# A decoder layer whose projections are moved between its expert steps: one tile in front, four and three behind

## The reference

```python
h = rms_norm(x, norm1_w) * (1 + sc1) + sh1            # sc, sh, g from silu(c) @ w_ada + b_ada
z = h @ w_in                                          # 1024 x 6656
q, k, v, u, gate_post, gate_pre, g_attn, g_conv = jnp.split(z, IN_SPLITS, axis=-1)
q, k = rms_norm(q, q_norm_w), rms_norm(k, k_norm_w)   # per head
o_attn = attend(q, k, v, sinks)                       # window of 128
conv_y = short_conv(gate_pre * u, conv_prev, conv_w, conv_bias)
merged = sigmoid(g_attn) * o_attn + sigmoid(g_conv) * (gate_post * conv_y)
x = x + g1 * (merged @ w_out)
h2 = rms_norm(x, norm2_w) * (1 + sc2) + sh2
x = x + g2 * peer_ffn(h2)                             # per token 8 heads x 16 rows of expert_u, expert_v
```

## Time and profile before

| | us |
|---|---|
| median of 3 runs | 3891.65 (3890.81 to 3892.19) |
| profiled execution, its own time | 3892.44 |
| its span | 3890.4 |
| PE busy | 3279.5 (84%) |
| DVE busy | 2530.7 (65%) |
| POOL busy | 2407.8 (62%) |
| ACT busy | 1077.4 (28%) |
| moved by DMA | 1259.47 MB, 324 GB/s over the span |

### The profile page before, as it was taken

How to read it: one execution, slowest core, us unless ns; L and a number is a source line. 1 busy time by engine, 2 the same in 40 slices (tenths; PEclk the granted TensorE clock), 3 DMA queues, 4 the chain that set the end, 5 groups by cost and what they waited for, 6 DMA issues and landing times.

```text
span 3890.4 us, 35676 instructions
## 1 busy us (share of the span) xinstructions
PE 3279.5 (84%) x10638; PEld 1724.2 (44%) x10638; DVE 2530.7 (65%) x5905; ACT 1077.4 (28%) x2400; POOL 2407.8 (62%) x2146
## 2 busy tenths in 40 slices
PE   4899995997999999999978778867887788789777
PEld 1457773444555655566534233423342334334221
DVE  2355546666887776787746677667766876776663
ACT  1225551222322322243212223213221323222220
POOL 1000003777667777766757777777777777776775
PEclk7999998999999999999989999999999999999999
DMA  6452225999999999999999999999999999999998
GB/s 217 160 172 71 60 60 186 345 373 382 367 356 371 385 384 351 390 353 348 357 392 363 370 358 351 363 358 365 372 365 360 372 369 376 368 374 336 370 364 316
DMA packets 466874, 1259.47 MB, mean 324 GB/s; under 512 B 42071, under 2 KB 171415, under 8 KB 466014
## 3 DMA queue, kind: packets, MB, share of 16 engines
q0 software_dynamic: 304128, 1107.43, 76.0%
q1 hardware_dynamic: 141290, 136.46, 10.7%
q10 hardware_dynamic: 21268, 13.32, 1.1%
HBM read 1238.54 MB, written 20.55 MB: 324 GB/s over the span
## 4 chain that ended last, share of the span: by engine, by line
PE 32%; DMA 25%; POOL 20%; DVE 9%; issue 9%; ACT 5%; SPq 0%; DVEq 0%; ACTq 0%; POOLq 0%
PE bank L1746 19%; DMA v_ring<-in_expert_v_dram,idx 18%; POOL u_ring L674 10%; POOL v_ring L682 10%; PE bank L1574 6%; DMA u_ring<-in_expert_u_dram,idx 5%; DVE u_ring L1349 2%; PE bank L1715 2%; PE bank L1770 1%; PE bank L1696 1%; DMA mod_s<-mod 1%; PE bank L1553 1%; ACT sm L768 1%; DVE rt L1132 1%; ACT sm L777 1%
## 5 line engine op out<-in xcount | busy, mean ns | idle before, releaser
L1746 PE MATMUL bank<-v_ring,diag 128*128 128x512 f32 (+1 forms) x4224 | 2068.8, 620 | 487.4 <-DMA v_ring<-in_expert_v_dram,idx 389.5
L1349 DVE CUSTOM_DVE_ANT_0 u_ring<-u_ring,h2b 128x1024 f32<-128x1024 f32 x1056 | 1286.8, 1225 | 877.7 <-DMA u_ring<-in_expert_u_dram,idx 835.9
L674 POOL DMA_INDIRECT u_ring<-in_expert_u_dram,idx x1056 | 1186.2, 1123 | 767.9 <-DVEq L1330 393.3
L682 POOL DMA_INDIRECT v_ring<-in_expert_v_dram,idx x1056 | 1206.4, 1142 | 475.1 <-PE bank L1746 239.9
L1746 PEld LDWEIGHTS bank<-v_ring,diag 128*128 128x128 f32 (+1 forms) x4224 | 754.0, 192 | 1555.6 <-DMA v_ring<-in_expert_v_dram,idx 830.5
L920 ACT ACTIVATE diag<-ident,wgt 128x128 f32<-128x128 f32 x1024 | 357.3, 394 | 664.2 <-PE bank L1746 310.1
L1574 PE MATMUL bank<-hi,whi 128*128 128x512 f32 x832 | 413.1, 497 | 2.4 <-issue 2.4
L1574 PE MATMUL bank<-hi,wlo 128*128 128x512 f32 x832 | 328.9, 395 | 0.0
L1574 PE MATMUL bank<-lo,whi 128*128 128x512 f32 x832 | 327.6, 394 | 0.0
L1126 DVE TENSOR_TENSOR wlo<-wc,whi 128x1024 fp32r<-128x1024 f32 x104 | 127.4, 1226 | 123.2 <-ACT whi L733 117.6
L1574 PEld LDWEIGHTS bank<-hi,whi 128*128 128x128 f32 x832 | 159.0, 191 | 75.5 <-issue 51.2
(11 more groups left out here) (259 smaller groups left out, 2607.4 us busy)
## 6 DMA issues: line engine op xcount, KB each, us to landing
wc<-in_w_in_dram SPq DMA_DIRECT2D x104, 512.0 KB, 5.9
ada_w<-in_w_ada_dram SPq DMA_DIRECT2D x12, 2048.0 KB, 8.1
u_ring<-in_expert_u_dram,idx POOLq DMA_INDIRECT x1056, 6.4
v_ring<-in_expert_v_dram,idx POOLq DMA_INDIRECT x1056, 6.4
wo_sb<-in_w_out_dram SPq DMA_DIRECT2D x2, 4096.0 KB, 19.1
wq_sb<-in_w_query_dram SPq DMA_DIRECT2D x2, 4096.0 KB, 28.1
xt<-in_x_prompt_dram SPq DMA_DIRECT2D x8, 512.0 KB, 4.9
out_dram<-h2b SPq DMA_DIRECT2D x8, 512.0 KB, 6.9
```

Source lines behind the costliest of these rows:

```text
L674: pool.indirect_dma_start(out=u_ring[k % RING][:, :], out_offset=None, in_=eu, in_offset=bass.IndirectOffsetOnAxis(ap=idx[n % IDXS][:, k:k ...
L682: pool.indirect_dma_start(out=v_ring[k % RING][:, :], out_offset=None, in_=ev, in_offset=bass.IndirectOffsetOnAxis(ap=idx[n % IDXS][:, k:k ...
L1349: V.tensor_tensor_reduce(out=u_ring[k % RING][:, :], in0=u_ring[k % RING][:, :], in1=h2b[t % 2][:, :], scale=1.0, scalar=0.0, op0=ALU.mult ...
L1746: last = M(banks(c, 1)[0:parts, :], diag[k % DIAGS][:, 0:parts], v_ring[k % RING][:, c * 512:(c + 1) * 512], start=first, stop=final)
```

## The change

The tiles are cut otherwise: tile 0 alone in front, then tiles 1 to 4, then tiles 5 to 7 together with the samples.

- **Front.** The first two sixths of the modulation are computed as columns (`modulation_columns`, four blocks of `w_ada` as stationary operand, 9 moving columns). Tile 0 is transposed before scale and shift. Its projection runs with its tokens stationary and the weights moving, 512 output columns at a time: 13 column blocks (`COLS1`), each of two units of 1 MB (`load_unit`, a ring of 3, split by `split_unit`), 12 matmuls a unit. The other eight `w_ada` blocks run one behind each of the first eight column blocks. The results are transposed back by `transpose_job`. Eight head pairs of attention, tile 0's convolution and the norms and transposes of tiles 1 to 4 run beside the column blocks 6 to 12.
- **Tiles 1 to 4** (group 0): the 52 blocks run in slots 0 to 69, one in 1.35 slots, all 24 matmuls in one slot. The weights have a ring of 3.
- **Tiles 5 to 7 and the samples** (group 1): the 52 blocks run in slots 280 to 558, one in 5.45 slots, in four pieces, with 416 moving columns; the separate 32-column matmuls are gone.
- **Attention** of tile 1 begins at slot 24, then 84, 142, 190, 500, 642, 770; the output steps of tiles 1 to 8 at 78, 142, 187, 233, 579, 690, 818, 930. Tiles 1 to 7 all go through DRAM for queries, keys, values and gates. Parked second inputs are those of tiles 3 and 4.
- `w_out` and `w_query` are loaded three times: at the end of the front, at slot 71 and at slot 571.

The core of the diff:

```diff
+COLS = 4
+HALF = KC // 2
+NUNIT = 2 * IN_W // ABLK
+UNIT_RING = 3
 NPROJ = QKV // P + 5 * KC
-NORMED = NQK // 2
...
-P2_LOAD = 98
-P2_SPLIT = 102
-P2_FIRST = 112
-P2_PITCH = 6.0
-A_MID = 330
-A_PITCH = 5
-MERGE_MID = 433
...
+GROUPS = ((1, 2, 3, 4), (5, 6, 7))
+NPT = tuple(len(g) * P for g in GROUPS)
+NTOK = (NPT[0], NPT[1] + NS)
+GMAX = max(NTOK)
...
+P_FIRST = (0, 280)
+P_PITCH = (1.35, 5.45)
+P_LOAD = (0, 266)
+NORM_AT, NORM_STEP = 266, 3
+WO_AT = (71, 571)
+ATTN = (None, 24, 84, 142, 190, 500, 642, 770)
+A_PITCH = (None, 4, 5, 4, 4, 5, 5, 5)
+MERGE = (None, 77, 135, 184, 231, 577, 688, 816)
+D_BASE = (None, 78, 142, 187, 233, 579, 690, 818, 930)
...
+SPLIT_HI, SPLIT_LO = (-3, -6), (-2, -4)
+PIECES = ((0,), (0, 1, 3, 4))
+SQUARE, MEANS, ROOT, NORM, PARK = (1, 5), (2, 6), (2, 7), (3, 8), (4, 10)
+BY_ACT, BY_DVE, TAPS, GATE, PARK_Y = (1, 5), (2, 6), (2, 7), (2, 7), (3, 9)
...
+        COLS1 = [("q", 0), ("q", 1), ("kv", 0), ("u", 0), ("pre", 0), ("u", 1), ("pre", 1),
+                 ("gc", 0), ("post", 0), ("gc", 1), ("post", 1), ("ga", 0), ("ga", 1)]
...
+            def load_unit(u):
+                if u >= UNIT_RING:
+                    sp.wait_ge(u_split, u - UNIT_RING + 1)
+                kind, c = COLS1[u // 2]
+                cols = slice(FIRST_COL[kind] + c * ABLK, FIRST_COL[kind] + c * ABLK + ABLK)
+                sp.dma_start(wu[u % UNIT_RING][:, :, :], w_in_v[:, u % 2 * HALF:u % 2 * HALF + HALF, cols]
+                             ).then_inc(wu_in[u % UNIT_RING], 16)
...
+            for i in range(len(COLS1)):
+                for u in (2 * i + 3, 2 * i + 4):
+                    if u < NUNIT:
+                        load_unit(u)
+                j = COLS - 1 + i
+                if COLS <= j < NBLK:
+                    if COLS + 2 <= j + 1 < NBLK:
+                        sp.wait_ge(mod_stored, 32 * (j - COLS))
+                        load_bias(j + 1)
+                    store_mod(j)
+                    if j + 2 < NBLK:
+                        load_ada(j + 2)
+                if i == 1:
+                    load_xt(1)
...
+            sp.wait_ge(u_split, NUNIT)
+            sp.wait_ge(pT_ps, KC)
+            sp.dma_start(wo_first[:, :, :], w_out_v).then_inc(wo_in, 16)
+            sp.wait_ge(unit_ps, NUNIT)
+            sp.dma_start(wq_first[:, :, :], w_query_v).then_inc(wq_in, 16)
...
+                for g in range(2):
+                    if s == WO_AT[g]:
+                        sp.wait_ge(proj_ps, (g + 1) * NPROJ)
+                        sp.dma_start(wo_sb[:, :, :], w_out_v).then_inc(wo_in, 16)
+                        if g:
+                            sp.wait_ge(new_stored, 32)
+                        sp.dma_start(wq_sb[:, :, :], w_query_v).then_inc(wq_in, 16)
+                        sp.wait_ge(gated, (g + 1) * KC)
...
+            def split_unit(u):
+                w(wu_in[u % UNIT_RING], 16 * (u // UNIT_RING + 1))
+                if u >= UNIT_RING:
+                    w(unit_ps, u - UNIT_RING + 1)
+                nc.scalar.copy(uhi[u % UNIT_RING][:, :, :], wu[u % UNIT_RING][:, :, :]).then_inc(uhi_made, 1)
...
+            for i in range(len(COLS1) + 1):
+                m, last = i - 6, i - 7
+                if i:
+                    columns(i - 1)
+                for u in (2 * i + 2, 2 * i + 3):
+                    if u < NUNIT:
+                        split_unit(u)
+                if 0 <= last < KC // 2:
+                    normalise(2 * last + 1, sm1[(2 * last + 1) % SM_RING])
+                if 0 <= m < KC // 2:
+                    exps(2 * m, sm1[2 * m % SM_RING])
+                if JOB_AT.get(i - 1, "")[0:1] == "x":
+                    keep_hT(int(JOB_AT[i - 1][1:]))
+                if i == 5:
+                    scale_x(1)
+                if i in (8, 10, 11):
+                    scale_x({8: 2, 10: 3, 11: 4}[i])
+                if i == 9:
+                    w(tr_ps, job("cu") + 1)
+                    link(nc.scalar.copy(cuT[:, :, 2:], banks(3, 2).rearrange("p (k t) -> p k t", k=KC)))
+                    act.sem_inc(tr_read, 1)
+                    act.sem_inc(cuT_made, 1)
+                if 0 <= m < KC // 2:
+                    normalise(2 * m, sm1[2 * m % SM_RING])
+                if 0 <= last < KC // 2:
+                    for p in (2 * last, 2 * last + 1):
+                        copy_pT(p, pT1[p % 2], 2)
+                if 0 <= m < KC // 2:
...
+            def modulation_columns(j):
+                w(ada_e_in[j], 16)
+                for c in range(ABLK // P):
+                    at = (j * ABLK // P + c) * (NB + 1)
+                    for k in range(KC):
+                        last = M(banks(5, 1)[:, at:at + NB + 1], ada_early[j][:, k, c * P:c * P + P], cT[:, k, :],
+                                 start=k == 0, stop=k == KC - 1)
+                last.then_inc(cols_ps, 1)
...
+            def column_matmuls(i):
+                if i >= 2:
+                    w(cb_by_dve, dve_cols(i - 2))
+                    w(cb_by_act, act_cols(i - 2))
+                if i == 0:
+                    w(lo_made, 1)
+                for u in (2 * i, 2 * i + 1):
+                    w(u_split, u + 1)
+                    r = u % UNIT_RING
+                    for k in range(HALF):
+                        at = u % 2 * HALF + k
+                        for x, wt in ((hi0, uhi), (lo0, uhi), (hi0, ulo)):
+                            last = M(banks(i % 2, 1), x[:, at, :], wt[r][:, k, :], start=at == 0 and (x, wt) == (hi0, uhi),
+                                     stop=at == KC - 1 and wt is ulo)
+                    last.then_inc(unit_ps, 1)
...
+            transpose_job("x0")
+            for j in range(COLS):
+                modulation_columns(j)
+            for i in range(len(COLS1)):
+                m, last, done = i - 6, i - 7, i - 8
+                if 0 <= m < KC // 2:
+                    scores_of(2 * m, aq[:, 2 * m, :])
+                column_matmuls(i)
+                if 0 <= done < KC // 2:
+                    weigh_values(2 * done + 1, pT1[1])
...
+                        for k, part in STEPS[piece * len(STEPS) // of:(piece + 1) * len(STEPS) // of]:
+                            last = M(banks(PBANKS[at % 3], 1)[:, 0:n], (wlo2 if part == 2 else whi2)[r][:, k, :],
+                                     (lo2 if part == 1 else hi2)[:, k, 0:n], start=(k, part) == (0, 0), stop=(k, part) == (KC - 1, 2))
```

More of the change, by code:

```diff
@@ new lines, in build @@
+        ada_w = ada_early[0:2]
+        mod = row(["mod0", "mod1"], 39064, ABLK)
+        mod_c = place("mod_c", 17080, 2 * KC, NB + 1)
+        A1c = place("A1c", 17224, KC, NB + 1)
+        r24c = place("r24c", 17296, 24)
+        cT = place("cT", 17320, KC, NB + 1)
+        xt, xh = row(["xt", "xh"], 12288, D)
+        hi0 = place("hi0", 14336, KC, P, dt=F32R)
+        lo0 = place("lo0", 15360, KC, P, dt=F32R)
+        hT0 = place("hT0", 15360, KC, P)
+        wu = row([f"wu{r}" for r in range(UNIT_RING)], 27776, HALF, ABLK)
@@ L231, in build @@
         sink_col = place("sink_col", 46680, NKV)
-        sm1 = row([f"sm1_{r}" for r in range(SM_RING)], 31872, 2, 2 * P)
-        pT1 = row(["pT1_0", "pT1_1"], 16384, 2, 2, P)
         sm2 = place("sm2", 47616, 2, 2 * P)
@@ L713, in row_rms @@
                 act.sem_inc(rms_made, 1)
+                w(rstd_made, t + 1)
+                link(nc.scalar.activation(h[0:parts, :], x[0:parts, :], ACT.Copy, scale=rstd[0:parts, :]))
+                act.sem_inc(xh_made, 1)
             def keep_hT(t):
[L716 to L720 removed]
```

1413 lines of the change are left out of this document (702 added, 711 removed).

## The result

The changed kernel takes 3956.4 us (median; 3951.4 to 3969.8), before 3891.9 beside it: ratio 1.0156, interval 1.0120 to 1.0191. It is slower by 64 us. The profiled execution has a span of 3959.1 us, 68.7 more than before.

What follows compares the result with a forecast made beforehand. Prediction: the front is PE bound, late slots DMA bound. Front -289.5, slots 0 to 70 +246.5, added bytes +44, coupling +10 make +11 on a span of 3890.4; forecast 3903 us, 8-in-10 range 3845 to 3980.

Steps and rivals of the forecast that it cites:

- The sign and the trade: Whole kernel: a PE-bound front exchanged for PE-bound slots and more bytes, without profit, 3903 us; chance of slower 0.56.
- The border of slot 71: Kernel before: slot 71 taken to start at 827 us, 67 dots counted as about 71 slots, some records missing.
- Start to the first column block: Front: four modulation blocks of 7.7 us end at 54, then scale, shift and split of tile 0, until 60 us.
- The steps of the front: Column blocks 0 to 7: a loop through SP sets iterations of 17.6 to 18.5 us, from 86 to 197 us.
- front at PE's pace: Front: units not held up behind the 2 MB load, iterations of 14.2 us, total 3871 us; chance 0.25.
- The tail of the front: Column blocks 8 to 12: 29, 16, 17, 13 and 25 us, to 297, given as 300 with some half clock.
- the third rival: Front: PE at half clock makes the kernel slower; chance 0.1.
- Slots 0 to 70: Tiles 1 to 4's projections make this stretch PE bound: 438 us instead of 191.5, bounds 409 and 485.
- The second rival: Slots 0 to 70: PE waits for splits and DVE for PE, 480 us there, total 3945; chance 0.2.
- Slots from 71 on: The other 985 slots are DMA bound: +44 us for 16.2 MB more, and net +10 for coupling.
- net "+10": Slots from 71: attention of tiles 3 and 4 over output steps +12, lighter second half 0 to -12, net +10 us.
- slots 142 to 220 clearly above 3.4 us: Sign of being wrong: these slots, where attention lies over output steps, were priced at PE 3.3 against DMA 3.1 us.

Runs made afterwards that it cites:

- e1: Changed kernel with the four early modulation blocks computed as rows of 512 columns plus 16 transposes instead of columns; ratio to before 1.0122, first output matmul 334.2 us instead of 357.7.
- e2: Changed kernel with the two 1 MB cache copies moved from the front's seventh step to slot 600; ratio to before 1.0183, first output matmul 351.1 us.
- e3: Changed kernel with the front's weight units issued one place further ahead; ratio to before 1.0115, first output matmul 335.9 us.
- e8: VectorE makes half the scaled transposes of tiles 1 to 4, against the kernel with three front repairs (modulation rows, late copies, units ahead); first output matmul 314.4 us in both.
- e11: Work for tiles 1 to 4 put behind tile 0's attention in late front steps, against the kernel with three front repairs; first output matmul 316.2 us against 314.4.
- e4: Changed kernel without the third product (8 of 24 matmuls a block) in tiles 1 to 4; ratio to before 1.0019, stage to slot 78 466.0 us for 523.9.
- e5: Changed kernel without the third product (8 of 24 matmuls a block) in tiles 5 to 7 and the samples; ratio to before 1.0151 against 1.0156.
- e10: Changed kernel with five slots a head pair instead of four for tile 3; ratio to before 1.0125, slots 78 to 276 take 661.0 us.
- e12: Five slots a head pair for tiles 2 to 4, against the kernel with three front repairs; ratio to before 1.0019, slots 78 to 276 take 653.7 us against 674.9.
- e6: Changed kernel with the output and query weights' reload at slot 71 cut to an eighth, 7.3 MB less; ratio to before 1.0118.

## Why the prediction was right or wrong

**The sign and the trade: right.** The kernel exchanged a front bound by TensorE for slots bound by TensorE plus more bytes, and lost a little. The time lies in the range. It is 53 us above the point given: a ratio of 1.0156 where 1.003 was forecast.

**The border of slot 71: misread, by 13 us, and luckily.** The prediction took 827 as the start of slot 71 and put the four dots lacking there down to missing records. None is missing: the line counts 1056 dots, one for each slot. At 827 the kernel before was at slot 67; slot 71 begins at 840.2, so slots 0 to 70 took 204.7 us, not 191.5. The sum replaces 191.5 us by 438 and keeps the other 13, which belong to the slots it replaces. Rightly bounded it gives 3890, no change. The sum so lies nearer to the measured time by an error, and that its point is slower than before rests on that error.

**Start to the first column block: failed, +25.** The step said that the four blocks done as columns cost what a block of rows does, 4 x 7.7 = 31 us, "half to twice". They take 54.6, all at the lower clock level (e1). Priced by their 256 weight loads at the upper level they come to about 29, an estimate, so the price of 31 would have been near; what failed is the clock under it, for which the step had no term. As rows, at the upper level from 28.4 us on, the product takes 29.7, and e1 gives 22.6 of the 25 back.

**The steps of the front: right in mechanism, short by 11.** From the first bias to the seventh it is 125.2 us against 111, and the step before the first bias was 3 shorter than forecast. The landings (11.2 to 11.6 us) are about those of the sum. What was overlooked stands in the diff: two copies of 1 MB in SP's seventh step. What the queue issues ahead of an awaited load was in the load's price here: e2 shows 18.5 instead of 11.0 us to landing and 6.1 us of time. The rival "front at PE's pace" did not come true; e3 shows that even with the units issued ahead the steps (15.0 to 20.9 us) stay above the 14.2 it took, since the ring of three is then what is waited for.

**The tail of the front: short by 22** (233.0 to 357.7 against 103 with the 3 us for the clock). e3 gives 8 of it back, and what it moves there is above all the last unit, which stood in SP behind the wait for taps and the loads of broadcast rows. The rest is the ping-pong of two head pairs a step, which the prediction priced by ScalarE's busy time alone; ScalarE was busy only 67.4 of 125 us. That the hand-overs between the engines make up the rest is read from the chain; e8 and e11 did not shorten it, and it stays open.

**Half clock in the front, the third rival: partly.** The granted clock is 0.87 in 95 to 250 and 0.75 in 233 to 358, with TensorE waiting between bursts, as in the earlier trace rows. In these windows it did not decide: TensorE was idle 39 of 155 us in the first and 53 of 125 in the last. It did where neither the rival nor the sum looked for it, in the modulation columns: by the estimate under e1 some 26 us (54.6 against about 29), nearly half of the miss of 58. After the change, as in the earlier trace rows, an activation starts right behind its table load, here 0.01 us behind a load of 1.28:

```profile
252.33 1.28 ACT L810 ACT_TABLE_LOAD   x1 [0.17 <-ACT esink L824]
253.62 0.60 ACT L810 ACTIVATE ug<-bank 128x512 f32<-128x512 f32 x1
```

**Slots 0 to 70: right in mechanism, 29 too long.** 408.6 us, at the floor of 409 and not at 438. TensorE is busy 300.0 of 300 us from 520 to 820. The 4% for waits and clock were not needed (clock 1.00), and of the 14 us in which VectorE was to be longer about 7 show (TensorE busy 73.1 of 80 us from 440 to 520). e4 confirms both halves. The second rival, coupling at 480, is out.

**Slots from 71 on: the bytes right, the coupling under-priced.** With the right border these slots took 3050.2 us before and take 3141.4 now: +91, where +54 was given. Of the +91, 42 lie in slots 71 to 77, 41 in slots 78 to 275, and 8 behind. The added bytes hold: the packets of the two traces sum to 1112.4 MB before and 1128.9 now, +16.5 where +16.2 was counted, and the longer slots 71 to 77 are paid for by the 15 MB more that they move. So the reload's waits, priced at 0, cost nothing beyond its bytes. The lighter second half brings nothing (e5), as taken.

What failed is the net "+10" with its "+12" for attention over output steps, where about 46 us are measured (91 less 45 for 16.5 MB). Slots 78 to 275 move less than before, 220 MB for 234, and still take longer, at 329 GB/s instead of 374. The sum looked at TensorE's busy time in a slot and not at the waits; the change also sets tiles 1, 3 and 4 at four slots a pair where all stood at five (`A_PITCH`, in the diff), and 9 to 21 us hang on that (e10, e12). The rest of the lower rate stays open. The sign of being wrong that the prediction named, "slots 142 to 220 clearly above 3.4 us", did come: 280.4 us for these 78 slots, 3.59 each, where before they took 3.21.

## What to carry to other kernels

Read the clock of a stretch from durations of a known form and not from a printed grant alone, above all at the start of a program. For a product with a very small operand, count the weight loads, compare both ways round, and price each at the clock level that its rows show; here turning it round took 29.7 us for 54.6. Check the border of a stage by counting its items: four dots lacking were four slots, not missing records. When a front is cut, look at what chain is left, here one of landings (11.2 to 11.6 us each) and hand-overs between engines: walk it in order, with every transfer that its queue issues on the way, since the busy time of any one engine said little here. And where a reused PSUM bank ties the next item to a copy of an earlier one, look at the pitch of the schedule: here it decided whether that copy was due in the same slot or long done, 25.6 us of waits against 5.0 (e10).

## What the runs showed of the hardware that was not expected

- 256 weight loads of 128x128, each with nine moving columns, ran from 23.7 to 78.1 us without a gap at 333 ns each, one every 0.213 us. Weight loads of this form last 333 ns at 341.8 to 344.3 us too, where the granted clock is 0.50, and 192 ns, one every 0.113 us, at 389.9 to 402.1, where it is 1.00. In e1, with 512 moving columns in the same place, the weight loads fall from 0.14 to 0.09 us at 28.4 us, and from one every 0.85 us to one every 0.43. For 23.7 to 78.1 us of the changed kernel, and for 24.2 to 28.4 of e1, 1.00 is printed all the same.
- A stop of TensorE and VectorE cost no more than its bytes while the queues ran full: 60 us at 383 GB/s behind slot 71, with 28.6 us of TensorE work. Cutting 7.3 MB of it took 20.5 us from the stage (e6).
